# Last pair of output tiles and first half of the next projection in two token halves, each half with a norm of its own

## The reference

```python
for layer in range(DEPTH):                      # DEPTH = 2
    h = rms_norm(x, norm_pre[layer])
    y = ab_mixer(h, ...) @ w_out  or  conv_mixer(h, ...) @ w_out
    x = x + rms_norm(y, norm_post[layer])
    h = rms_norm(x, xattn_norm_pre[layer])
    y = memory_cross_attention(h, m, m_w_q, m_w_kv, m_w_o)
    x = x + rms_norm(y, xattn_norm_post[layer])

def rms_norm(x, gain):                          # mean over the 2048 features of one token
    return x * rsqrt(mean(x * x, -1) + EPS) * gain
```

## Time and profile before

| | |
|---|---|
| time, median of 3 runs | 2444.67 us (2441.99 to 2446.73) |
| the profiled execution's own time | 2447.89 us |
| its span, first to last instruction | 2446.1 us |
| mean granted TensorE clock | 0.992 |
| PE busy | 2390.0 us (98%) |
| DVE, ACT, POOL busy | 1293.2, 810.4, 229.0 us |

### The profile page before, as it was taken

How to read it: one execution, slowest core, us unless ns; L and a number is a source line. 1 busy time by engine, 2 the same in 40 slices (tenths; PEclk the granted TensorE clock), 3 DMA queues, 4 the chain that set the end, 5 groups by cost and what they waited for, 6 DMA issues and landing times.

```text
span 2446.1 us, 29636 instructions
## 1 busy us (share of the span) xinstructions
PE 2390.0 (98%) x11652; PEld 1985.7 (81%) x11652; DVE 1293.2 (53%) x1722; ACT 810.4 (33%) x1376; POOL 229.0 (9%) x160
## 2 busy tenths in 40 slices
PE   7999999999999999999999999999999999999998
PEld 6788888888777778988877788888888888888777
DVE  5566666664555557643385682443333343433755
ACT  4232323232443437532244432212212221322434
POOL 3010101010010101011130420000000000011400
PEclk9999999999999999999999999999999999999999
DMA  6622323343433434452321223332323332233222
GB/s 173 106 70 62 83 61 83 60 77 68 129 87 74 82 78 130 142 186 89 101 69 61 84 89 103 103 95 78 113 91 103 98 99 86 95 103 121 69 69 86
DMA packets 237517, 229.81 MB, mean 94 GB/s; under 512 B 22384, under 2 KB 230768, under 8 KB 237424
## 3 DMA queue, kind: packets, MB, share of 16 engines
q1 hardware_dynamic: 237280, 228.00, 33.9%
q10 hardware_dynamic: 144, 0.52, 0.1%
HBM read 223.52 MB, written 4.98 MB: 93 GB/s over the span
## 4 chain that ended last, share of the span: by engine, by line
PE 86%; DVE 7%; issue 3%; ACT 2%; DMA 1%; POOL 0%; SPq 0%; DVEq 0%; ACTq 0%; POOLq 0%
PE acc L884 22%; PE acc L886 22%; PE acc L885 22%; PE acc L1213 2%; PE acc L1214 2%; PE acc L1218 2%; DVE weights_lo L1350 1%; PE m L1033 1%; DVE work L1831 1%; PE acc L1086 1%; PE acc L1087 1%; PE acc L1088 1%; PE m L963 1%; ACT weights_hi L464 1%; PE m L1041 1%
## 5 line engine op out<-in xcount | busy, mean ns | idle before, releaser
L884 PE MATMUL acc<-input_hi,weights_hi 128*128 128x512 f32 (+1 forms) x2776 | 1092.2, 393 | 20.0 <-DVE weights_lo L1350 17.0
L886 PE MATMUL acc<-input_hi,weights_lo 128*128 128x512 f32 (+1 forms) x2776 | 1070.1, 385 | 0.0
L885 PE MATMUL acc<-input_lo,weights_hi 128*128 128x512 f32 (+1 forms) x2776 | 1069.4, 385 | 0.0
L1350 DVE TENSOR_TENSOR weights_lo<-weights_raw,weights_hi 128x1024 fp32r<-128x1024 f32 x400 | 533.8, 1349 | 323.0 <-ACT weights_hi L464 321.9
L884 PEld LDWEIGHTS acc<-input_hi,weights_hi 128*128 128x128 f32 x2776 | 523.3, 189 | 134.3 <-DVE weights_lo L1350 18.1
L464 ACT ACTIVATE weights_hi<-weights_raw 128x1024 fp32r<-128x1024 f32 x400 | 418.5, 1057 | 625.7 <-PE acc L886 570.8
L886 PEld LDWEIGHTS acc<-input_hi,weights_lo 128*128 128x128 f32 x2776 | 522.7, 188 | 105.4
L885 PEld LDWEIGHTS acc<-input_lo,weights_hi 128*128 128x128 f32 x2776 | 523.5, 189 | 99.8 <-issue 1.9
L2044 POOL TENSOR_TENSOR small<-small 128x4 f32<-128x4 f32 (+1 forms) x19 | 25.4, 1337 | 826.5 <-DVE small L1580 378.0
L1775 DVE COPY work<-acc 128x512 f32<-128x512 f32 x48 | 31.1, 684 | 125.9 <-PE acc L886 115.4
L2106 POOL TENSOR_TENSOR work<-work 128x512 f32<-128x512 f32 x42 | 54.4, 1295 | 335.0 <-ACT work L742 332.0
(11 more groups left out here) (283 smaller groups left out, 2222.5 us busy)
## 6 DMA issues: line engine op xcount, KB each, us to landing
weights_raw<-in_ab_w_in SPq DMA_DIRECT2D x128, 512.0 KB, 5.2
weights_raw<-in_c_w_in SPq DMA_DIRECT2D x128, 512.0 KB, 3.8
weights_raw<-in_m_w_kv SPq DMA_DIRECT2D x32, 512.0 KB, 3.3
weights_raw<-in_ab_w_out SPq DMA_DIRECT2D x32, 512.0 KB, 4.4
weights_raw<-in_m_w_q SPq DMA_DIRECT2D x32, 512.0 KB, 3.3
weights_raw<-in_c_w_out SPq DMA_DIRECT2D x32, 512.0 KB, 4.3
residual<-in_x SPq DMA_DIRECT2D x32, 256.0 KB, 4.9
weights_raw<-in_m_w_o SPq DMA_DIRECT2D x16, 512.0 KB, 3.3
```

What stands on the lines that cost most here:

```text
L884: pe.matmul(out, w_hi[:, o:o + P], hi(kt), start=kt == 0, stop=False)
L885: pe.matmul(out, w_hi[:, o:o + P], lo(kt), start=False, stop=False)
L886: last = pe.matmul(out, w_lo[:, o:o + P], hi(kt), start=False, stop=kt == last_kt)
L1350: TTO(w_lo[:, s * CW:(s + 1) * CW], raw[:, c * CW:(c + 1) * CW], w_hi[:, s * CW:(s + 1) * CW].bitcast(F32), ALU.subtract).then_inc(lo_read ...
```

## The change

- The last pair of output tiles is computed for tokens 0 to 255 first (part 0, over all its chunks) and then for tokens 256 to 511 (part 1), with matmuls of 256 columns. A bank now holds one token half of both tiles. Its chunks are released in part 1 only.
- Squares of tiles 12 and 13 get places of their own, and PE sums tiles 12 to 15 directly instead of through POOL. `whole_sums` stands inside part 0, `last_sums(r, part)` and `norm_rows(r, part)` follow each half. For r = 0 and 2, half 0's stand inside part 1; half 1's stand inside the opening.
- Norm work on tiles 0 to 7 is done in halves: first all of half 0 (names with "a"), then all of half 1 ("b"). Tiles 8 to 15 stay whole.
- The opening's tiles 0 to 7 run as four blocks (q, n) for half 0 and then four for half 1, each 4 tiles x 2 banks x 3 matmuls of 256 columns. Tiles 8 to 15 are as before.
- `split`s of the next projection's first four chunks get places by hand among this work.

The core of the diff:

```diff
-ACT_AHEAD, VECTOR_AHEAD = (1, 6, 7, 11, 12), (5, 8, 9, 13, 14)
+ACT_AHEAD, VECTOR_AHEAD = (8, 9, 11, 13), (9, 10, 12, 14)
+HALF, EARLY = T // 2, 8
...
+        sqt = lambda k: cq[:, (k % 2 if k < 12 else k - 12) * T:((k % 2 if k < 12 else k - 12) + 1) * T]
+        token_half = lambda part: slice(part * HALF, (part + 1) * HALF)
+        last_half = lambda t, part: t.rearrange("p (j n) -> p j n", j=2)[:, :, token_half(part)]
+        row_bank = lambda part: M[1 + part]
...
+            def last_square(r, part, pair):
+
+                act.wait_ge(*((chunk_used, done_at(pair)) if part else NM("y0", r)))
+                act.activation(last_half(cq[:, 2 * T:4 * T], part), head2(bank(pair, part)), ACT.Square)\
+                    .then_inc(*OA.did(f"s14{part}"))
...
+                if per == 1:
+                    for c in range(3):
+                        split(c0 + 8 + c)
+                last_square(r, 0, p0 + 7)
+                if per == 1:
+                    last_square(r, 1, p0 + 7)
+                    split(c0 + 8 + 3)
+                else:
+                    for c in range(2):
+                        split(c0 + 8 * per + c)
...
+                for k in range(2, EARLY):
+                    high(k, "a", token_half(0))
+                    if k == 3:
+                        split(c0 + 2)
+                    if k == 4 and r != 1:
+                        last_square(r, 1, last)
+                    if k == 6:
+                        split(c0 + 3)
...
+            def last_sums(r, part):
+
+                pe.wait_ge(*OA(f"s14{part}", r))
+                for k in (14, 15):
+                    last = ss_part(sqt(k), False, (2 * part, 2 * part + 1))
+                last.then_inc(*NM.did(f"ss{part}"))
+
+            def norm_rows(r, part):
+
+                pe.wait_ge(*NG(f"pow{part}", r))
+                rows(lambda t: row_bank(part)[:, t * P:(t + 1) * P], lambda t: powed[:, t:t + 1], 2 + 2 * part)\
+                    .then_inc(*NM.did(f"rows{part}"))
+
+            def whole_sums(r):
+
+                pe.wait_ge(*OG("a11", r))
+                ss_part(acc_sq, True)
+                for k in (12, 13):
+                    pe.wait_ge(*OA(f"s{k}", r))
+                    ss_part(sqt(k), False)
+
+            def last_pair(g, pair, per, r):
+
+                pe.wait_ge(acc_free, 2 * (pair - 1))
+                for part in range(2):
+                    for c in range(per):
+                        s = (g + c) % SPLIT_SLOTS
+                        if part == 0:
+                            pe.wait_ge(lo_ready, g + c + 1)
+                        for j in range(2):
+                            out = bank(pair, part)[:, token_half(j)]
+                            for k in range(4):
+                                kt, o = 4 * c + k, s * CW + k * 256 + j * P
+                                hi, lo = (H[:, kt * T:(kt + 1) * T][:, token_half(part)] for H in (H_hi, H_lo))
+                                pe.matmul(out, w_hi[:, o:o + P], hi, start=j == 0 and kt == 0, stop=False,
+                                          skip_group_check=True)
+                                pe.matmul(out, w_hi[:, o:o + P], lo, start=False, stop=False, skip_group_check=True)
+                                last = pe.matmul(out, w_lo[:, o:o + P], hi, start=False, stop=kt == 4 * per - 1,
+                                                 skip_group_check=True)
+                            if part and j:
+                                last.then_inc(chunk_used, 1)
+                            elif j and c == per - 1:
+                                last.then_inc(*NM.did("y0"))
+                            if part == 0 and c == per - 1 and j == int(per == 1):
+                                whole_sums(r)
+                            if part and (c, j) == (0, 0):
+                                last_sums(r, 0)
+                            if part and (c, j) == ((1, 0) if per > 1 else (0, 1)):
+                                norm_rows(r, 0)
...
+                for part, tag in enumerate("ab"):
+                    for q, n in ((0, 0), (0, 1), (1, 0), (1, 1)):
+                        if part == 0:
+                            pe.wait_ge(lo_ready, c0 + 2 * q + n + 1)
+                            if q == 0:
+                                pe.wait_ge(acc_free, 2 * (p0 - 1 + n))
+                        for k in range(4):
+                            kt = 4 * q + k
+                            hi, lo = (H[:, kt * T:(kt + 1) * T][:, token_half(part)] for H in (H_hi, H_lo))
+                            at_ = [((c0 + 2 * q + n) % SPLIT_SLOTS) * CW + k * 256 + j * P for j in range(2)]
+                            out = [bank(p0 + n, j)[:, token_half(part)] for j in range(2)]
+                            if n == 0:
+                                pe.wait_ge(*(NA(f"hi{kt}{tag}", r) if kt > 1 else NV(f"hi{kt}{tag}", r)))
+                            for j in range(2):
+                                pe.matmul(out[j], w_hi[:, at_[j]:at_[j] + P], hi, start=part == 0 and kt == 0, stop=False,
+                                          skip_group_check=True)
+                                pe.matmul(out[j], w_lo[:, at_[j]:at_[j] + P], hi, start=False, stop=False,
+                                          skip_group_check=True)
+                            if n == 0:
+                                pe.wait_ge(*NV(f"lo{kt}{tag}", r))
+                            for j in range(2):
+                                last = pe.matmul(out[j], w_hi[:, at_[j]:at_[j] + P], lo, start=False, stop=False,
+                                                 skip_group_check=True)
+                        if part:
+                            last.then_inc(chunk_used, 1)
+                        elif q == 0:
+                            (last_sums, norm_rows)[n](r, 1)
...
+                take_last(r, 0)
+                stat_of(0)
+                if r == 1:
+                    take_last(r, 1)
+                    split(c0 + 3)
+                else:
+                    split(c0)
+                for part, end in enumerate((EARLY, KT)):
+                    tile_ = lambda k: (k, "ab"[part] if k < EARLY else "", token_half(part) if k < EARLY else slice(0, T))
+                    if part:
+                        split(c0 + 3)
+                        stat_of(1)
+                    dve.wait_ge(*NM(f"rows{part}", r))
+                    scaled(*tile_(0))
+                    whole(*tile_(0))
+                    scaled(*tile_(1))
+                    scaled(*tile_(2))
+                    whole(*tile_(1))
+                    if part == 0:
+                        split(c0 + 1)
+                    for k in range(3, end + 2):
+                        if k == EARLY and part:
+                            dve.wait_ge(acc_free, 2 * (P_OUT0 + 8, P_O0 + 8, P_OUT1 + 8)[r])
+                        if k < end:
+                            scaled(*tile_(k))
+                        if k == 3 or k > 4:
+                            low(*tile_(k - 1 if k == 3 else k - 2))
+                        if part:
+                            split_ahead(split, VECTOR_AHEAD, k, c0)
+                        elif k == 5 and r != 1:
+                            take_last(r, 1)
+                        elif k == 6:
+                            split(c0 + 2)
...
+                for part, tag in enumerate("ab"):
+                    o = slice(2 * part, 2 * part + 2)
+                    pool.wait_ge(*NV(f"stat{part}", r))
+                    pool.tensor_tensor(powed[:, o], stat[:, o], minus_half[:, o], ALU.pow).then_inc(*NG.did(f"pow{part}"))
+                    for k in range(2, EARLY):
+                        added(k, tag, token_half(part))
+                for k in range(EARLY, KT):
+                    added(k, "", slice(0, T))
```

183 lines of the change are left out of this document (72 added, 111 removed).

## The result

| | before | changed |
|---|---|---|
| median of the runs, us | 2445.49 (2441.99 to 2446.73, 4 runs) | 2466.7 (2464.79 to 2473.05, 4 runs) |
| ratio to the kernel before | 1 | 1.0093, 95% interval 1.0079 to 1.0106 |
| profiled execution: own time, span, us | 2447.89, 2446.1 | 2468.28, 2466.3 |
| passages 0, 1, 2, us | 76.88, 62.50, 75.67 | 79.52, 70.37, 81.06 |
| their sum, us | 215.05 | 230.95 |

The account below looks back on a forecast made before the run. PE bounds the kernel, busy 2390.0 of 2446.1 us. Waits 7.0 + 6.6, late weights 3.9 and clock 4.0 make 21.5, less 8.5 won: 13.0 us slower, median 2457.5 us; 8-in-10 range 2446 to 2470.

Parts of the forecast that it names:

- Halving: Last pairs and openings: two 256-column matmuls replace each of 504, costing 0.0133 us each, 6.7 us.
- Sums: PE sums tiles 12 to 15 one by one, 40 records a passage: 4.8 us each, 14.3 us in three.
- Waits in passages 0 and 2: PE waits before half 1's rows in the opening for half 1's power: 3.5 us, twice.
- DVE's count: Passages 0 and 2, DVE's work from half 0's rows to half 1's power input: 16.0 us, done at 36.7.
- Late weights: Openings: slots released late and splits among whole tiles delay weights, 1.3 us a passage (0 to 2), 3.9 us.
- Waits in passage 1: PE idles 3.9 us before half 0's first scaled operands, and block (0,0) ends 2.7 us later (1 to 4).
- Clock: Low clock from sum records and waits: 1 us each in passages 0 and 2, 2 in passage 1; 4 us.
- more than 15 us at 0.50 in a passage: Sign of being wrong: PEclk at 0.50 over more than 15 us of a passage, pointing to rival 2.
- rival 2: The clock falls in every passage and stays low as long as now: 26 us slower, 2471 us; chance 0.19.
- The sum by passage: Forecast length of passages 0, 1 and 2: about 80.2, 67.5 and 80.2 us.
- The time of all else unchanged: Expected sign in the changed profile: everything outside the three passages takes the same time.
- What a clean version could give: If PE never waited and kept its clock in the passages, the change would win 8.5 us.

Follow-up runs that it names:

- experiment 5: Changed kernel, but POOL adds squares of tiles 12 and 13 again (8 sum records in a row for 24; passage 1's block one place later): 2456.2 us, ratio 1.0046.
- experiment 6: Kernel before, with 16 unused one-column sum records more behind POOL's sum in each last pair: 2452.8 us, ratio 1.0031 to the kernel before.
- experiment 1: Changed kernel, with half 1's rows moved behind block (1,0) of half 0 in passages 0 and 2: 2467.7 us, ratio 1.0088 to the kernel before.
- experiment 4: Changed kernel, half 1's rows behind block (1,0) in passages 0 and 2, and ACT's half of four splits one tile earlier: 2462.5 us, ratio 1.0075.
- experiment 9: Changed kernel, with passage 1 written as in the kernel before on all engines; 0 and 2 stay in halves: 2461.2 us, ratio 1.0072.
- experiment 8: Changed kernel; in passage 1 DVE copies half 1 and splits behind the scaling of half 0's first two tiles: 2465.5 us, ratio 1.0089.
- experiment 10: Changed kernel, passage 1 as before; in 0 and 2 POOL adds tiles 12 and 13, half 1's rows later, ACT's splits earlier: 2452.3 us, ratio 1.0031.
- experiment 2: Changed kernel, half 1's rows behind block (1,0) in passages 0 and 2, DVE's mean of squares for half 1 ahead of its split: 2465.9 us, ratio 1.0091.
- experiment 3: Changed kernel, with ACT's half of four splits one tile earlier and DVE's order kept: 2460.2 us, ratio 1.0068 to the kernel before.
- experiment 7: Kernel before, with only the 504 matmuls each issued as two of 256 columns back to back, same weights: 2460.4 us, ratio 1.0065.

## Why the prediction was right, and where it wasn't

The side, the size within the range, the waits and their places were right; the time was 9 us short. By its steps:

- **Halving**, 6.7: right. 0.120 us apart; alone 5.3 in the passages, where in passage 1 a shorter wait takes back 0.2.
- **Sums**, 14.3, of which 5.7 are the 16 records more in each passage: the price is right to 0.1, 1.8 us for 16 in passage 0 by experiments 5 and 6. The 5.7 us in all of experiment 6 agree by luck, since a wait hid the records in passage 1 and low clock came on top.
- **Waits in passages 0 and 2**, 3.5 us each: 3.47 and 3.48, at the rows, released by the power, the mean right behind a split. DVE's count was 16.0 us, and it took 15.9 in passage 0; it gave half 1's power at 37.6, and PE's rows came at 37.3. What I had wrong is what the wait is worth. I took it as lost time that an edit could give back. Experiments 1 and 4 show that it was cover: the ring over DVE, POOL and ACT, which the prediction did not see, ends at the same time with or without it.
- **Late weights**, 1.3 a passage: 1.33 in passage 1 and none to speak of in 0 and 2. What hid them there is the 3.4 us of low clock behind the wait, which held PE up instead: with the same wait and the clock at 1.00, passage 0 of experiment 9 has 0.63 and 0.71. I had them as a side effect of slots freed late; the cause is the ring, 5.95 us a turn against PE's 5.44.
- **Waits in passage 1**, 3.9 and 2.7: 3.37 and 0.66. The places were right, the second was too large. What the first is worth stays open, since experiment 8 only moved it.
- **Clock**, 4 in all, of it 2 in passage 1: mis-sized there. Passage 1 was at 0.50 for 20.5 us, against 10.2 before; half of 10.3 is 5 us. In 0 and 2 it was 3.4 and 6.8 us, less than or as long as before. The prediction named more than 15 us at 0.50 in a passage as its sign of being wrong, in favour of rival 2; passage 1 passed it, 0 and 2 did not. The sum by passage: +2.6, +7.9, +5.4 for the predicted +3.3, +5.0, +4.5. That 0 and 2 come so near is in part luck: late weights of 1.3 us each stayed away, and low clock behind the wait (in 2 behind the sums too) stood in for them.
- **"The time of all else unchanged"**: wrong. 4.4 us of the profile's 20.2, and 5.1 if counted from 533 us, is the transfer ahead of passage 0 that landed later, behind late weights.

So 15.9 us of passages against 13.0, the surplus chiefly in passage 1's clock, and 4.4 us that lie ahead of them: together the profile's 20.2. By the medians it is 21. What a clean version could give was 8.5 us by my sum; experiment 10 gave 1.0 in passages 0 and 2 together, where a tail of 40.3 us and a shorter wait at the rows stayed, and 0.0 over all three, since passage 1 took 1.0 more.

Open: why the loads of weights ahead of the write of `block_inverses` take longer to land in kernels whose code up to there is the same as before; and what makes the clock fall in passage 1. How long it stays low there follows from when it falls: with 24 records it came back 24.5 to 24.8 us into the passage where it had fallen only behind the wait for the first `H_hi` (10.2 us, experiments 2 to 4), and at 27.1 to 27.4 where it had fallen right behind the sums (20.5 us: changed, 1 and 8). Why it fell early in three kernels and late in three others, whose code for passage 1 is the same up to that point, no run shows.

## What to carry to other kernels

A wait in front of the busiest engine is worth removing only if nothing else ends at the same time: measure the distance from the wait to a fixed point behind it over several places, and if it is the same everywhere, look for a ring of engines that sets it. A ring shows as equal idle times, one for each turn, each engine waiting for the next; one entry moved by one place in one engine's order can break it. Splitting work to start a dependent chain earlier has a price that is sure (here 14 us for the halves and for 20 records more in each passage) against a gain that the chain's own engines must be able to take up.

## What the runs showed of the hardware

- The clock fell from 1.00 to 0.50 at the end of 24 sum records of one column or up to 1.5 us behind them in 9 of 20 such blocks, with no wait of PE ahead of it: in passages 1 and 2 of the changed kernel and in passage 0 of experiment 2, for instance. In passage 0 of the changed kernel the same 24 records left it at 1.00: the same code can keep or lose the clock. The Trainium skill (TensorE: Matmul & The Clock Gate, HAM oscillation) tells of idle gaps between groups of matmuls that put the clock back; the trace agrees where 3.4 us at 0.50 follow the 3.47 us wait, but in these nine places no gap stood ahead.
- The wait of 3.47 us at half 1's rows went with low clock in 8 of 10 places (changed, experiments 3, 5, 8 and 9); in passage 2 of experiment 5 and passage 0 of experiment 9 the clock stayed at 1.00.
- Records of one column start 0.112 us apart at 1.00 and 0.213 at 0.50. That is nearly what a matmul of 256 columns takes (0.120 and 0.213).
- Two matmuls of 256 columns that use the same weights back to back cost no less than two with different ones: 0.120 us each (experiment 7 and the earlier trace rows).
- A power of two columns on POOL takes 0.71 us, and 1.62 where a split ran beside it on DVE (passages 0 and 2 of experiment 2).
- A write of 128 KB in packets of 64 bytes took 4.9 us in two executions of one kernel and 7.6 in another kernel with the same code up to there, where its first packet started 2.6 us later, while packets of a load of weights ahead of it in the queue, 13.9 us for 11.2, were still moving. Kernels can differ by 0.2% in a place that the change doesn't touch, so a difference of that size needs the profile to say where it lies.
